# Reordering the delta stage: grams, turns and decay products moved, decay products on VectorE, base blocks sent from ScalarE's queue

## What the reference computes

```
g = cumsum(g)                                   # log-decay, inside a chunk
decay = exp(where(i >= j, g_i - g_j, -inf))
a_low = where(i > j, (beta k) k^T * decay, 0)
tmat  = inverse(I + a_low)                      # unit lower triangular
u, w  = tmat (beta v), tmat (beta k exp(g))
qk    = q k^T * decay
scan over chunks:
    v_new = u_i - w_i S
    o_i   = (q_i exp(g)) S + qk_i v_new
    S     = S exp(g_last) + k_dec_i^T v_new
```

## Time and profile before

| | |
|---|---|
| median of 3 runs | 3491.55 us (3489.17 to 3492.2) |
| the profiled execution's own time | 3483.28 us |
| its span, first to last instruction | 3481.5 us |
| mean granted TensorE clock | 0.979 |
| busy: PE, DVE, ACT, POOL | 3277.5, 1448.9, 1002.4, 1350.0 us |

### The profile page before, as it was taken

How to read it: one execution, slowest core, us unless ns; L and a number is a source line. 1 busy time by engine, 2 the same in 40 slices (tenths; PEclk the granted TensorE clock), 3 DMA queues, 4 the chain that set the end, 5 groups by cost and what they waited for, 6 DMA issues and landing times. The chain is left out here.

```text
span 3481.5 us, 51024 instructions
## 1 busy us (share of the span) xinstructions
PE 3277.5 (94%) x20680; PEld 2703.7 (78%) x20680; DVE 1448.9 (42%) x2240; ACT 1002.4 (29%) x1720; POOL 1350.0 (39%) x1166
## 2 busy tenths in 40 slices
PE   6999999999797979899999999999799999999998
PEld 5888888777687868787788878878688877777877
DVE  4333333353545444456733332333472044444343
ACT  3444434522343434311211101111222133432221
POOL 4222222243425252435433333334434355554543
PEclk9999999999899989999999999999899999999999
DMA  2000100112101010213111111111321111111122
GB/s 107 31 31 31 37 31 31 37 43 84 49 19 49 26 48 20 72 66 151 62 49 44 48 48 48 48 42 49 124 83 45 49 42 51 47 45 49 60 85 79
DMA packets 104199, 188.06 MB, mean 54 GB/s; under 512 B 32329, under 2 KB 64713, under 8 KB 101329
## 3 DMA queue, kind: packets, MB, share of 16 engines
q1 hardware_dynamic: 104016, 185.48, 16.3%
HBM read 158.33 MB, written 27.12 MB: 53 GB/s over the span
## 5 line engine op out<-in xcount | busy, mean ns | idle before, releaser
L303 PE MATMUL DP<-XH,WH 128*128 128x512 f32 x2592 | 831.0, 402 | 23.4 <-POOL WL L251 23.4
L249 POOL CAST WH<-WRAW 128x1024 fp32r<-128x1024 f32 (+2 forms) x258 | 266.4, 1032 | 1504.0 <-issue 892.4
L303 PE MATMUL DP<-XL,WH 128*128 128x512 f32 x2592 | 804.6, 392 | 0.0
L303 PE MATMUL DP<-XH,WL 128*128 128x512 f32 x2592 | 803.1, 391 | 0.0
L251 POOL TENSOR_TENSOR WL<-WRAW,WH 128x1024 fp32r<-128x1024 f32 (+2 forms) x258 | 588.5, 2281 | 20.8
L303 PEld LDWEIGHTS DP<-XH,WL 128*128 128x128 f32 x2592 | 488.5, 188 | 105.6
L303 PEld LDWEIGHTS DP<-XL,WH 128*128 128x128 f32 x2592 | 488.6, 188 | 104.9
L303 PEld LDWEIGHTS DP<-XH,WH 128*128 128x128 f32 x2592 | 467.1, 189 | 125.2 <-issue 26.4
L871 DVE SCALAR_TENSOR_TENSOR SS<-B,RQ,SBI 128x256 f32<-128x256 f32 (+2 forms) x192 | 74.4, 429 | 314.8 <-PE B L570 314.8
L380 DVE TENSOR_TENSOR XR<-XR,B 128x1024 f32<-128x1024 f32 x88 | 106.5, 1220 | 101.7 <-PE B L360 101.7
L721 ACT ACTIVATE PP<-SS,NM 128x256 f32<-128x256 f32 (+2 forms) x192 | 88.8, 464 | 178.7 <-DVE NM L878 178.7
(11 more groups left out here) (479 smaller groups left out, 5140.9 us busy)
## 6 DMA issues: line engine op xcount, KB each, us to landing
WRAW<-in_w_up SPq DMA_DIRECT2D x44, 512.0 KB, 3.5
WRAW<-in_w_attn SPq DMA_DIRECT2D x36, 512.0 KB, 3.5
WRAW<-in_w_down SPq DMA_DIRECT2D x22, 512.0 KB, 3.4
XR<-in_x SPq DMA_DIRECT2D x8, 1024.0 KB, 8.4
WRAW<-in_w_dn SPq DMA_DIRECT2D x16, 512.0 KB, 3.6
aa_dram<-AA SPq DMA_DIRECT2D x12, 512.0 KB
YY<-yy_dram SPq DMA_DIRECT2D x12, 512.0 KB, 3.9
WRAW<-in_w_lrux SPq DMA_DIRECT2D x10, 512.0 KB, 3.4
```

Source lines behind the costliest of these rows:

```text
L249: pool.tensor_copy(WH[b.slot][:, 0:b.kt, :], WRAW[b.slot][:, 0:b.kt, :]).then_inc(w_hi, 1)
L303: mm = pe.matmul(DP[b.slot][:, half * H:half * H + H], w[b.slot][:, k, :], x[:, k, half * H:half * H + H], start=one, stop=end)
```

## The change

In words, with p the pair:

- `spread` moves from POOL to VectorE. There it is four `tensor_scalar` instructions of 128 x 128 a group (before: two of 128 x 256 on POOL). VectorE does two groups at a time (`next_spreads`): groups 0 and 1 ahead of the pairs; 8p+2 and 8p+3 during the dense products; 8p+4 and 8p+5 at q = 2 of round 0; 8p+6 and 8p+7 at q = 7 of round 0; 8p+8 and 8p+9 at q = 3 of round 1.
- Of the first two groups, `gram(8p, 0)` goes from step 5 to step 4 of the v product, `gram(8p, 1)` from step 2 of z to step 7 of v; `turn_a` from steps 4 and 5 to steps 1 and 2 of z. `spread_g` of groups 8p+2 and 8p+3 goes from behind z into step 5 of z, and `gram(8p+2, 0)` from q = 0 of round 0 to behind z.
- In round 0 the turns and `take_a` of 8p+2, 8p+3 (round 1's matrices) go from q = 2 to q = 1. The preparation of 8p+6, 8p+7 (round 3's) begins in round 0 (q = 9, 10, 11) and ends in round 1 with the turns at q = 2 instead of q = 5.
- The write of `AA` to DRAM moves from SP's queue to ScalarE's (`blocks_out`), right behind the `take_a` that completes it, and `aa_dram` is two buffers used in turn. SP keeps the other transfers.

The diff, cut to its core:

```
 BL, BY, BT, BW = (at(n, 124 + i, [P, 16, 16]) for i, n in enumerate(("BL", "BY", "BT", "BW")))
-aa_dram = nc.dram_tensor("aa_dram", [8, P + 1, P], F32, kind="Internal").ap()
+aa_dram = [nc.dram_tensor(f"aa_dram{i}", [8, P + 1, P], F32, kind="Internal").ap() for i in range(2)]
...
 NGRP = NPAIR * NT
-aa_out, blk_in, yy_out, yy_in, blk_step, blk_ready = sel_in, bias_in, cm_in, con_in, x0_part, og_sum
-AA0, BLK0, YYO0, YYI0, RDY0 = 16, 16, 32, 32, 2 * NPAIR
+aa_out, blk_in, yy_out, yy_in, blk_step, blk_ready = (sel_in, st_t), bias_in, cm_in, con_in, x0_part, og_sum
+AA0, BLK0, YYO0, YYI0, RDY0 = (16, 6), 16, 32, 32, 2 * NPAIR
...
 def grp(n):
...
 def blocks_sp(sp, g):
...
-    c, v, m = chain(g), g % 2, g % 4
-    sp.wait_ge(aa_ready, 2 * g + 2)
-    sp.dma_start(matrices(aa_dram), AAV[m][:, :, :, :, :].rearrange("p d e h n -> p (d e h) n")).then_inc(aa_out, 16)
-    sp.wait_ge(aa_out, AA0 + 16 * (c + 1))
+    c, v = chain(g), g % 2
+    sp.wait_ge(aa_out[c % 2], AA0[c % 2] + 16 * (c // 2 + 1))
...
     for d, t in enumerate((BL, BY)):
-        sp.dma_start(t[32 * d:32 * d + 32, :, :], diagonal(aa_dram, d)).then_inc(blk_in, 16)
+        sp.dma_start(t[32 * d:32 * d + 32, :, :], diagonal(aa_dram[c % 2], d)).then_inc(blk_in, 16)
...
                  matrices(yy_dram)).then_inc(yy_in, 16)
+
+def blocks_out(act, g):
+
+    c, m = chain(g), g % 4
+    act.wait_ge(aa_ready, 2 * g + 2)
+    if c >= 2:
+        act.wait_ge(blk_in, BLK0 + 32 * (c - 1))
+    act.dma_start(matrices(aa_dram[c % 2]), AAV[m][:, :, :, :, :].rearrange("p d e h n -> p (d e h) n")).then_inc(
+        aa_out[c % 2], 16)
...
 def both_parts(n, d, h):
...
         def hook(k):
...
                 square_sums(p, 0)
+            if k == 4:
+                gram(NT * p, 0)
             if k == 5:
-                gram(NT * p, 0)
+                square_sums(p, 1)
             if k == 7:
-                square_sums(p, 1)
+                gram(NT * p, 1)
...
     def during_z(p):
         def hook(k):
+            if k == 1:
+                turn_a(NT * p)
             if k == 2:
-                gram(NT * p, 1)
+                turn_a(NT * p + 1)
...
                 turn_o(p - 1)
-            if k == 4:
-                turn_a(NT * p)
             if k == 5:
-                turn_a(NT * p + 1)
+                spread_g(NT * p + 2)
+                spread_g(NT * p + 3)
...
         if m == 0:
-            if q in (0, 1):
-                gram(n, q)
-            if q == 3:
-                spread_g(n + 2)
-                spread_g(n + 3)
+            if q == 0:
+                gram(n, 1)
+            if q in (3, 9):
+                i = 2 if q == 3 else 4
+                spread_g(n + i)
+                spread_g(n + i + 1)
...
                 gram(n + 2, q - 5)
-            if q in (2, 7):
-                i = 0 if q == 2 else 2
+            if q == 11:
+                gram(n + 4, 0)
+            if q in (1, 7):
+                i = 0 if q == 1 else 2
...
                 turn_a(n + i + 1)
-        if m == 1:
-            if q == 1:
-                spread_g(n + 2)
-                spread_g(n + 3)
-            if q in (3, 4):
-                gram(n + 2, q - 3)
-            if q == 5:
-                turn_a(n + 2)
-                turn_a(n + 3)
+        if m == 1 and q == 0:
+            gram(n + 2, 1)
+        if m == 1 and q == 2:
+            turn_a(n + 2)
+            turn_a(n + 3)
...
         product(pe, Block("dn", p, 3), XH, XL, within=during_z(p))
-        spread_g(NT * p + 2)
-        spread_g(NT * p + 3)
+        gram(NT * p + 2, 0)
...
         if m == 0:
-            if q == 4:
-                exponential(n + 2)
-                exponential(n + 3)
-            if q in (2, 7):
-                i = 0 if q == 2 else 2
+            if q in (4, 11):
+                i = 2 if q == 4 else 4
+                exponential(n + i)
+                exponential(n + i + 1)
+            if q in (1, 7):
+                i = 0 if q == 1 else 2
...
                 take_a(n + i + 1)
-        if m == 1:
-            if q == 2:
-                exponential(n + 2)
-                exponential(n + 3)
-            if q == 5:
-                take_a(n + 2)
-                take_a(n + 3)
+                blocks_out(act, 4 * p + 1 + i // 2)
+        if m == 1 and q == 2:
+            take_a(n + 2)
+            take_a(n + 3)
+            blocks_out(act, 4 * p + 3)
...
         conv_silu(p, 1)
+        root(p, 1)
         conv_mid(p, 2)
-        root(p, 1)
-        conv_silu(p, 2)
...
         take_a(NT * p + 1)
+        conv_silu(p, 2)
+        exponential(NT * p + 2)
+        exponential(NT * p + 3)
...
         take_y0(NT * p + 1)
-        exponential(NT * p + 2)
-        exponential(NT * p + 3)
...
 def delta_dve(dve):
+    def spread(n):
+
+        p, s, e, v = grp(n)
+        if n >= 2:
+            dve.wait_ge(dec_ready, 4 * (n // 2))
+        for d in range(2):
+            for h in range(2):
+                x = dve.tensor_scalar(RB[e][:, d, h, :], con("tri", d, P), ABN[:, chunk(s, d), 8 * d + 2 * p + h:
+                                                                              8 * d + 2 * p + h + 1], None, ALU.mult)
+        x.then_inc(rb_ready, 1)
+
+    def next_spreads(n):
+        for i in (n, n + 1):
+            if i < NGRP:
+                spread(i)
+
...
         if m == 0:
-            if q in (0, 1):
-                decayed(n, q)
-                decayed(n + 1, q)
+            if q == 0:
+                decayed(n, 1)
+                decayed(n + 1, 1)
+            if q == 2:
+                next_spreads(n + 2)
...
                 decayed(n + 3, q - 5)
+            if q == 7:
+                next_spreads(n + 4)
+            if q in (9, 10):
+                exponents(n + q - 5)
+            if q == 11:
+                decayed(n + 4, 0)
+                decayed(n + 5, 0)
         if m == 1:
-            if q in (1, 2):
-                exponents(n + q + 1)
-            if q in (3, 4):
-                decayed(n + 2, q - 3)
-                decayed(n + 3, q - 3)
-
+            if q == 0:
+                decayed(n + 2, 1)
+                decayed(n + 3, 1)
+            if q == 3:
+                next_spreads(n + 4)
+
+    dve.wait_ge(mm_done, last_block("attnout"))
+    dve.wait_ge(abn_ready, 1)
+    next_spreads(0)
...
         decayed(NT * p + 1, 0)
-        taps(p, 2)
...
         decayed(NT * p + 1, 1)
+        next_spreads(NT * p + 2)
+        taps(p, 2)
...
             o_out(p - 1)
+        exponents(NT * p + 2)
+        exponents(NT * p + 3)
...
         dve.wait_ge(st_zero, p + 1)
-        exponents(NT * p + 2)
-        exponents(NT * p + 3)
+        decayed(NT * p + 2, 0)
+        decayed(NT * p + 3, 0)
...
 def delta_pool(pool):
-    def spread(n):
-
-        p, s, e, v = grp(n)
-        if n >= 2:
-            pool.wait_ge(dec_ready, 4 * (n // 2))
-        for d in range(2):
-            i = 8 * d + 2 * p
-            g = ABN[:, chunk(s, d), i:i + 2].rearrange("p (h k) -> p h k", k=1).broadcast_to([P, 2, P])
-            x = pool.tensor_tensor(RB[e][:, d], twice(con("tri", d, P)), g, ALU.mult)
-        x.then_inc(rb_ready, 1)
-
...
         pool.wait_ge(blk_step, step(p, c, 1))
-        pool.wait_ge(rb_ready, min(NT * p + 2 * (g % 4) + 4, NGRP))
...
     split_first(pool, "dn")
-    pool.wait_ge(mm_done, last_block("attnout"))
-    pool.wait_ge(abn_ready, 1)
-    spread(0)
-    spread(1)
...
         split(pool, Block("dn", p, 3))
-        for i in range(2, 4):
-            spread(NT * p + i)
...
         for m in range(1, 4):
-            for n in range(NT * p + 2 * m + 2, min(NT * p + 2 * m + 4, NGRP)):
-                spread(n)
```

## The result

| | before | after |
|---|---|---|
| median | 3491.88 us (3489.17 to 3495.04, 4 runs) | 3449.38 us (3442.38 to 3458.65, 4 runs) |
| profiled execution: own time, span | 3483.28, 3481.5 us | 3442.38, 3440.5 us |
| mean granted clock | 0.979 | 0.986 |
| busy: PE, DVE, ACT, POOL | 3277.5, 1448.9, 1002.4, 1350.0 us | 3274.9, 1478.2, 1011.9, 1311.7 us |

The changed kernel is faster: ratio 0.988, 95% interval 0.9855 to 0.9905. The prediction was 3452 us (3437 to 3473). TensorE's busy time hardly moved; what went is idle time.

The account below looks back on a forecast made before the run. TensorE's idle waits for `YY`, set by the spacing of its loads, were taken as the bound. Per pair -1.8 - 4.9 - 4.5 + 2.0 = -9.2, four pairs -36.8, start -2.5: -39.3 us, giving 3452 us (3437 to 3473).

Parts of the forecast that it names:

- the hand-over changes nothing: Rival, chance 0.05: early `AA` brings blocks no sooner, as `YY`'s buffer or POOL holds every chain; 3488 us.
- First chain, -1.8: Round 0 to round 1: `AA` out 2.9 us earlier in a round beginning 1.1 later, so 1.8 us less a pair.
- Second chain, -4.9: First to second `YY` load: bound by round 1's second `scan2`, 19.8 us against 24.7, a pair.
- the 1.6 us of low clock: Round 1 ahead of its second `scan2`: low clock after the first wait expected to go, 1.6 us less.
- the 2.3 us that I allowed: Each chain: 2.3 us from the end of POOL's work to the issue of the `YY` load.
- Third chain, -4.5: Second to third `YY` load: POOL's chain sets the pace, 19.2 us against 23.7, a pair.
- Collision, +2.0: VectorE's decay products and POOL's chains hold each other up: 1.0 us for each of two chains a pair (0 to 4).
- Start of the stage, -2.5: TensorE's 3.01 us wait for the first spread shrinks with VectorE making it: 2.5 us less, between -5 and -0.5.
- The gram that I moved ahead of round 0 (+1.1): Ahead of round 0 TensorE gets one more gram, so the round begins 1.1 us later.
- Everything overlaps: Rival, chance 0.18: no collision, and blocks land 2 us sooner behind `YY`; 14.8 us less, 3437 us.
- The small load is stuck behind `YY`: Rival, chance 0.17: blocks come only behind `YY`'s landing, another 2 us; 17.6 us more, 3470 us.
- VectorE becomes the bound: Rival, chance 0.07: decay products at 0.9 us each delay VectorE's list in the level loops; slower, 3504 us.

Follow-up runs that it names:

- order_only_spq: The changed kernel with the write of `AA` back in SP's queue, two buffers kept: 3481.22 us, ratio 0.9958 to the kernel before.
- queue_only: The kernel before with only the `AA` write moved to ScalarE's queue and two buffers, no step moved: 3495.53 us, ratio 0.9997.
- Write_later: The changed kernel with the second `AA` written at q = 11 of round 0 in place of q = 7: 3456.91 us, ratio 0.9893.
- after_again: The changed kernel unchanged, timed again beside other runs: 3456.17 us, ratio 0.9888 to the kernel before.
- Turn_early: The changed kernel with round 3's turns, `take_a` and write at q = 1 of round 1 in place of q = 2: 3452.11 us, ratio 0.9877.
- fetch_first: Turn_early with the third chain's blocks fetched ahead of the second `YY` load in SP's list: 3447.49 us, ratio 0.9879.
- third_buffer: fetch_first with round 3's `YY` placed where round 1's `AA` lay, its load waiting only for round 2's first `scan2`: 3443.23 us, ratio 0.9865.
- products_pool: The changed kernel with the decay products back on GpSimd, all else kept: 3459.18 us, ratio 0.9904.

## Why the prediction was right, and where it was not

**The cause.** Two things held the chains: `AA` was ready late for round 1, and behind SP's wait for rounds 2 and 3. The experiments show that most of the gain needs both: 0 for the products alone, 0 for the queue alone, 15 us for the order with the products, 40 us for all on the same chip. The rival "the hand-over changes nothing" fell with order_only_spq. queue_only shows the mechanism: whoever is freed first meets the next limit, `YY`'s buffer and then a late third `AA`.

**First chain, -1.8.** From round 0 to round 1 it is 32.7 us and was 34.9, -2.1 where my terms make -2.9. Right in its parts: `AA` out at 6.87 (7.1), fetch 3.2 behind, GpSimd 2.8 behind that, 12.3 us of chain. One step was missed: the small writes of the blocks landed 1 us late, since the second `AA`, sent earlier, was in flight. Write_later, where that write leaves later, shows it. And round 0's own work ended at 1056.44, 30.4 us after its start, where I had 31.6. (My 1070.5 is 32.7 us after the old start, not the 32 written beside it.) So the first wait was 2.3 us and not under 1.5, and the waits of a pair came to 6.5 us on average, not 5.

**Second chain, -4.9.** Measured -3.5 (21.2 us and not 19.8). The term that failed is the 1.6 us of low clock that I struck off: the wait ahead of round 1 stayed, the clock fell again, and the second `scan2` stood 15.76 us into the round, not 14.2. That `scan2` bounds this load was right (issue at 1075.69, `scan2` ends at 1075.61). In the first pair of after_again the clock stayed up and `scan2` stood at 14.2, as I had summed it; but the load came 22.7 us behind the first all the same and not 19.8. So a second term was too small: the 2.3 us that I allowed from the end of GpSimd's chain to the load is 5.8 there, since the third `AA`, sent 0.35 us ahead, was in flight beside the small write. I had asked of the new writes only what their issue costs ScalarE.

**Third chain, -4.5.** Measured -4.4 (19.3 us; 19.2 predicted), though I had the fetch 0.5 behind the load and it came 2.05 behind. It cost little: the blocks then reach GpSimd 3.0 us behind the fetch and not 4.3. That GpSimd's chain sets the pace was right, in all four pairs. Turn_early and fetch_first show a second bound close by that I had not given for this chain, the second `scan2` of round 2; third_buffer removes both and the wait is gone.

**Collision, +2.0.** Mis-sized. Four of GpSimd's 32 steps (not 33) rose by 0.06 to 0.07 us, 0.3 us in the first chain, and a call on VectorE from 1.65 to 1.86. The second and third chain lasted 12.0 us, as without products beside them. It is +0.3 a pair at most, and by products_pool the whole move is worth about 1 us of the period at most, either way. So the +2.0, which was nearly empty, stood against the 0.8 and 1.4 us that the first two chains missed: from round 0 to round 3 my terms make -10.3 us, and pair 1 shows -9.9 (the mean of the four pairs -10.7). That the sum is right is partly these two errors cancelling. One `tensor_scalar` took 0.28 us, not 0.22, but a call of eight took 1.65 us, near the 1.8 that the sum used, since they follow one another every 0.21 us.

**Start of the stage, -2.5.** Measured -1.1: VectorE was held to the end of GpSimd's split, the condition that I had named. The gram that I moved ahead of round 0 (+1.1) shows as +0.7 on average: from round 3 to the next round 0 it is 82.7 us and was 82.0. But that mean mixes the levels of the clock: behind a low clock at the start of round 3, as it was in all three before (0.50 to 0.61 over 4 us), it is 83.2 and 83.3, so +1.2; where the clock stayed up it is 81.7. The upper end of the forecast's own range is 3462 by its terms, not 3463.

**The other rivals.** "Everything overlaps": the collision was indeed near nothing, but 3437 was missed by the first and second chain. "The small load is stuck behind `YY`": GpSimd started 4.28 us behind the fetch (4.45 predicted), not 6.4. "VectorE becomes the bound": it needed 0.75 us an instruction, and eight took 1.65 to 1.88 us in the loops.

## What to carry to other kernels

When a chain of transfers is late, write down for each link every condition that it waits for and when each is met. Here the second and third load had three within a few microseconds of each other (GpSimd's chain, the buffer, the landing of a small write beside a large one), and an edit that moved one alone was worth little or nothing. A transfer that waits for nothing but stands behind a queue's semaphore wait is late for no reason: give it to an engine that has just finished its data. But look at what the path waits for at the moment when it will be in flight: sent just ahead of a small write, it cost up to 3.5 us. And a wait that is shortened but not removed may keep its full price in clock.

## What was not expected of the hardware

- A VectorE instruction of 0.28 us took 2.375 us (the longest of its 128), beside a GpSimd `tensor_tensor` of 2.41 us. It was the same with `tensor_tensor` on VectorE (0.418 us by the median, 2.586 the longest). In the other direction GpSimd's steps were stretched by some 0.07 us.
- A write of 32 KB issued 2.4 to 2.7 us behind a write of 512 KB on another queue let the next step go 2.9 to 3.2 us after its issue, issued 0.35 us behind one 5.4 to 5.5 us after, and 1.9 us without one.
- The 32 KB loads behind a 512 KB load on the same queue: GpSimd started 4.3 us behind the first, where it is 2.8 otherwise.
- A wait of 2.2 to 2.5 us ahead of round 1 was followed by 1.2 GHz in all four pairs of the changed kernel's first profile, sometimes at once and once 1 us into the round (there the first `times_a` still took 1.18 us, but the clock was 0.62 over 4 us). In the first pair of both repetitions it was not, after 2.40 and 2.24 us. The length of the wait does not decide it: in third_buffer the clock stayed at 1.00 after 2.56 us and fell to 0.50 after 2.54. What does, no run here explains.
